# Products of constants around the norm sums of a two-block transformer kernel, in PSUM areas that nothing reads

## What is computed

```
def rms_norm(x, g):
    xf = x.astype(jnp.float32)
    y = xf * lax.rsqrt(jnp.mean(xf * xf, axis=-1, keepdims=True) + EPS)
    return y.astype(x.dtype) * g
...
    def pre(t, mm, i, gi):
        return rms_norm(t, g[gi]) * (1 + mm[:, :, i + 1]) + mm[:, :, i]

    def post(t, y, mm, i, gi, wres):
        return t + wres * mm[:, :, i + 2] * rms_norm(y, g[gi])
...
    for i in range(DEPTH):
        h = _rmsnorm(x, norm_g[i, 0])
        ...
        x = x + _rmsnorm(h, norm_g[i, 1])
        f = _conv_ffn(_rmsnorm(x, norm_g[i, 2]), ffn_w_up[i], ffn_conv_w[i], ffn_conv_b[i], ffn_w_down[i])
        x = x + _rmsnorm(f, norm_g[i, 3])
```

## Time and profile before

| | |
|---|---|
| median of three runs | 2756.01 us |
| profiled execution | 2758.69 us, its span 2756.9 us |
| TensorE matmul records | 2623.8 us busy, 95% of the span |
| VectorE (DVE), ScalarE (ACT) | 1558.1 us and 1185.0 us |
| mean granted TensorE clock | 0.977 of full speed |
| DMA | 375.51 MB, mean 136 GB/s |

### The profile page before, as it was taken

The page is one execution under the profiler, slowest core; times in us unless marked ns, Lnnn a source line. Parts: engine busy times, 40 slices in busy tenths (PEclk is TensorE's granted clock), DMA queues, the critical chain, the costliest instruction groups (busy, mean ns, idle before and its releaser), DMA issues. The chain is left out here.

```text
span 2756.9 us, 38954 instructions
## 1 busy us (share of the span) xinstructions
PE 2623.8 (95%) x16089; PEld 2250.3 (82%) x16089; DVE 1558.1 (57%) x2180; ACT 1185.0 (43%) x1636; POOL 112.5 (4%) x174
## 2 busy tenths in 40 slices
PE   6999999999999998999999989989988899898998
PEld 4777786876677786888886879989977899887998
DVE  5777536455777634322336574456566676565675
ACT  4222226454422224422326454444556565453663
POOL 1111300000111000000200000000000000000000
PEclk9999999999999999999999999999999999899999
DMA  8666532212566523223423234544421455331553
GB/s 304 230 225 227 137 107 62 62 62 84 172 216 212 194 92 97 71 93 112 123 77 92 62 115 159 179 157 144 166 80 55 134 182 180 137 127 62 172 172 114
DMA packets 248077, 375.51 MB, mean 136 GB/s; under 512 B 9820, under 2 KB 188568, under 8 KB 247936
## 3 DMA queue, kind: packets, MB, share of 16 engines
q1 hardware_dynamic: 228592, 300.56, 32.7%
q0 software_dynamic: 18768, 70.85, 7.9%
q10 hardware_dynamic: 576, 2.10, 0.2%
HBM read 372.34 MB, written 1.16 MB: 135 GB/s over the span
## 5 line engine op out<-in xcount | busy, mean ns | idle before, releaser
L499 PE MATMUL ps<-uh,wh 128*128 128x256 f32 (+1 forms) x4128 | 1382.8, 335 | 53.5 <-DVE ul L896 32.6
L500 PE MATMUL ps<-ul,wh 128*128 128x256 f32 (+1 forms) x4128 | 1366.2, 331 | 0.0
L501 PE MATMUL ps<-uh,wl 128*128 128x256 f32 (+1 forms) x4128 | 1365.9, 331 | 0.0
L499 PEld LDWEIGHTS ps<-uh,wh 128*128 128x128 f32 x4128 | 792.5, 192 | 169.0 <-issue 54.6
L501 PEld LDWEIGHTS ps<-uh,wl 128*128 128x128 f32 x4128 | 792.3, 192 | 71.3
L500 PEld LDWEIGHTS ps<-ul,wh 128*128 128x128 f32 x4128 | 793.0, 192 | 67.9 <-issue 0.7
L490 DVE TENSOR_TENSOR wl<-ring,wh 128x2048 fp32r<-128x2048 f32 (+1 forms) x209 | 475.1, 2274 | 479.8 <-ACT wh L485 376.1
L485 ACT ACTIVATE wh<-ring 128x2048 fp32r<-128x2048 f32 x155 | 296.7, 1915 | 712.5 <-PE ps L501 708.9
L1238 DVE TENSOR_TENSOR wl<-ring,wh 128x2048 fp32r<-128x2048 f32 x66 | 151.3, 2292 | 300.4 <-ACT uh L1256 281.7
L762 DVE SCALAR_TENSOR_TENSOR arena<-arena,act_c 128x384 f32<-128x384 f32 x420 | 228.5, 612 | 88.0 <-DMA arena<-in_w_ada_dram 87.7
L1235 ACT ACTIVATE wh<-ring 128x2048 fp32r<-128x2048 f32 x66 | 126.4, 1915 | 335.7 <-PE ps L501 335.7
(11 more groups left out here) (367 smaller groups left out, 2198.5 us busy)
## 6 DMA issues: line engine op xcount, KB each, us to landing
ring<-in_ffn_wi_dram SPq DMA_DIRECT2D x88, 1024.0 KB, 7.5
arena<-in_w_ada_dram POOLq DMA_DIRECT2D x84, 768.0 KB, 5.4
ring<-in_ffn_w_up_dram SPq DMA_DIRECT2D x44, 1024.0 KB, 7.0
ring<-in_ffn_wo_dram SPq DMA_DIRECT2D x20, 2048.0 KB, 8.0
ring<-in_ab_w_in_dram SPq DMA_DIRECT2D x13, 2048.0 KB, 7.6
ring<-in_ffn_w_down_dram SPq DMA_DIRECT2D x10, 2048.0 KB, 7.7
ring<-in_c_w_in_dram SPq DMA_DIRECT2D x6, 2048.0 KB, 8.0
ring<-in_w_in_dram SPq DMA_DIRECT2D x20, 512.0 KB, 6.5
```

What stands on the lines that cost most here:

```text
L499: pe.matmul(to, sh, mh, start=start and n == 0, stop=False)
L500: pe.matmul(to, sh, ml, start=False, stop=False)
L501: mm = pe.matmul(to, sl, mh, start=False, stop=stop and last)
```

## The change

A method `keep_busy` issues n products of the ones matrix with 256 columns of constants (the identity and the ones matrix). `Norm.tensor` calls it ahead of the sums unless the stage has begun with other products (the latent ones pass `begun=True`): six with 512 columns, into bank 2, four with 256 columns, into columns 256 to 511 of bank 7. With 512 columns it calls it again behind the sums, six into bank 0. Nothing reads the results. Since DVE still reads columns 0 to 255 of bank 7 with 256 columns, its multiply for k = 7 waits until the four are done. The method `done` counts the new semaphore on.

```diff
+        kept_busy = signal("products_between_done")
...
+            def keep_busy(self, pe, bank, n):
+
+                for _ in range(n):
+                    mm = pe.matmul(bank, ones, const[:, 0:S], start=True, stop=True)
+                return mm
+
-            def tensor(self, pe):
+            def tensor(self, pe, begun=False):
                 if self.post is None:
                     return
+                if not begun:
+                    if self.n_s == 2:
+                        self.keep_busy(pe, ps[:, 2, 0:S], 6)
+                    else:
+                        self.keep_busy(pe, ps[:, KD - 1, S:T2], 4).then_inc(kept_busy.sem, 1)
                 for k in range(KD):
                     pe.wait_ge(h_squared.sem, h_squared.at(k + 1))
                     last = pe.matmul(self.sum_bank(), ones, self.sq[:, k, :], start=(k == 0), stop=(k == KD - 1))
                 last.then_inc(sum_ready.sem, 1)
+                if self.n_s == 2:
+                    self.keep_busy(pe, ps[:, 0, 0:S], 6)
...
-                    self.post.vector(dve)
+                    self.post.vector(dve, (lambda: dve.wait_ge(kept_busy.sem, kept_busy.at(1))) if self.n_s == 1 else None)
...
-            def vector(self, dve):
+            def vector(self, dve, last_bank_free=None):
                 T = self.T
                 dve.wait_ge(y_rstd.sem, y_rstd.at(1))
                 for k in range(KD):
+                    if k == KD - 1 and last_bank_free is not None:
+                        last_bank_free()
...
-                    norm.tensor(pe)
+                    norm.tensor(pe, begun=True)
```

More of the change, by code:

```diff
@@ L928, in done @@
                 if self.post is not None:
+                    if self.n_s == 1:
+                        kept_busy.passed(1)
                     h_squared.passed(KD + 1)
```

## The result

| | before | after |
|---|---|---|
| median | 2756.35 us (8 runs, 2754.86 to 2761.11) | 2764.31 us (8 runs, 2757.56 to 2768.88) |
| ratio to before, 95% interval | | 1.0026 [1.0017, 1.0034] |
| profiled execution, span | 2758.69, 2756.9 us | 2765.02, 2763.2 us |
| mean granted clock | 0.977 | 0.984 |

The account below looks back on a forecast made before the run. The prediction took a stream of matmuls as the bound, with time lost where TensorE idles or runs at 1.2 GHz. Sums 3.0 plus wide first products 1.5 gave 4.5 us, hence 2751.5 us; 8-in-10 range 2746.5 to 2757.

Parts of the forecast that it names:

- Cost of the products: At the boundaries' gaps: 56 constant products, some 25 us of TensorE, fit into idle time; 0 on the path.
- DVE's wait: Ahead of DVE's eighth multiply (k = 7) at 256-column boundaries: the four products are done long before; cost 0.
- Sums: Sums at the nine boundaries: shorter idle ahead keeps the clock more often; gain 3.0 us, between 0 and 4.8.
- First products, wide: After the sums at 512-column boundaries: idle 4.68 becomes 2.0, three quarters of 2.1 us kept; gain 1.5, between -2.8 and 2.1.
- First products, narrow: After the sums at 256-column boundaries: 2.7 us idle stays, three of five lose the clock again; 0, between +4.1 and -2.8.
- rival C: 256-column boundaries: clock loss moves to the first products of all five, +2.8 us there; total about 2760 us; chance 0.10.
- C's other half: 256-column boundaries: the last sums still run at half speed, so the 3.0 us is not gained.
- Other clock losses: Dense work untouched by the change: clock losses can begin a little earlier or later; 0, plus or minus 1.5 us.
- the two places with narrow weight-bound products: 2398.60 to 2405.40 us, after products 32 columns wide with full TensorE records, and a like place near 1900.
- the three times shown: Run times of the kernel before, spread over only 2.5 us, taken to speak for a small part of chance.

## Why the prediction was wrong, point by point

**Cost of the products, DVE's wait: right.** 2.8 us for six, all in the gaps; the first product comes 4.64 us after the start of the Ln at boundary 2, as before, and the first sum 4.48 us after the end of the residual's sum, as before. No squares were late.

**Sums: the size nearly right, with two errors in it.** The term was 3.0. The Ln's wait fell by all of 5.0 us (15.3 to 10.3): the clock held under every sum, at the projections too, where I had given it three fifths. But at 6 and 8 the end of the sums is not what is late next. DVE at boundary 6, after:

```profile
1851.04 1.23 DVE L1770 TENSOR_TENSOR wl<-ring,wh 128x1024 fp32r<-128x1024 f32 x1
1852.17 2.29 DVE L491 TENSOR_TENSOR wl<-ring,wh 128x2048 fp32r<-128x2048 f32 x1
1854.37 1.28 DVE L903 SCALAR_TENSOR_TENSOR arena<-h,cols,rstd 128x256 f32<-128x256 f32 x3
```

Two pieces of weight splitting stand on DVE between the last update of `h` and the scaling, and end at 1854.4; 1/rms would have been there at 1853.4. Before, the slow sums hid them. Of 1.45 and 0.97 us gained, 0.96 went back at each; net 3.1. TensorE's idle stretch ahead of the first products grew by the same amount there, from 2.75 to 3.71 us. All 20 such places without products behind the sums lost their clock, ten with some 2.8 us of idle time and ten with 3.7.

**First products, wide: 1.5 forecast, 1.4 in the profile, at most 0.6 of it by the change.** Boundary 1 gave 0.8 and boundary 2 0.6. But at boundary 1 the 49th product starts 12.8 us after the first in the changed kernel, in the second profile of the unchanged program, and with nine products behind the sums at a clock of 1.00. So the 13.6 us of the profile on which the forecast rests were an unlucky case, and the change has no share in that gain. All that boundaries 1 and 2 gained, 0.8 and 0.6 in first products and 0.85 in sums, was given back at once: the stage between boundaries 2 and 3 took 375.3 us before and 377.5 after. TensorE's wait there for the modulation tiles that DVE folds, in the window 712:1086 of before and 709:1086 of after:

```profile
PE ps L778 <- DVE arena L762: 0.2, 1, 0.2
```

```profile
PE ps L779 <- DVE arena L763: 2.4, 4, 0.9
```

The seven profiles with products at the wide boundaries have 376.2 to 377.5 us in this stage, the six without them 374.9 to 375.7. That DVE and the loads of the modulation weights set a pace of their own there, for which an earlier TensorE waits, fits these numbers; no run tested it. The kernel with wide products alone made no difference in time (1.0005). And the products kept the clock less often than the three quarters I gave: in six profiles with six behind the sums, 16 of 24 wide boundaries still had low clock in their first products; with nine, none of four.

**First products, narrow: 0 forecast, +4.3 in the profile.** This step failed, and rival C named it, with a chance of 0.10 and 2.8 us. The forecast took which boundaries lose their clock to be drawn anew, three of five again. It is not drawn: in all five profiles without products at the narrow boundaries it is 5, 6 and 8 that lose, never 7 or 9. With four products ahead and none behind (five profiles), 5, 6 and 8 lost 14 of 15 times and 7 and 9 four of ten, 18 of 25 in all; the changed kernel's profile, with all five, is the worst of them (the others have three, three, three and four), and a loss there can cost more, 2.6 us at boundary 7. Four products behind removed most of it: 2 of 10 lost, both at projections, where 2.0 us of idle time were left (1.0 at the others), and 8.3 us in the median. C's other half, that the sums would stay slow, was wrong.

**Other clock losses: 0 plus or minus 1.5 forecast, +4.1 in the scans and +1.2 between 8 and 9.** This is the second step that failed, and the larger one. By the sizes in the profile, either loss alone leaves the median outside the range (2759.0 without this one, 2760.0 without the last); without both it would be 2754.7. I had seen that clock losses in dense work could start "a little earlier or later", and priced that by the two places with narrow weight-bound products; the scans I took as fixed. The three kernels that move nothing but the scans' start show the size: 0.9 us of added work made one 6.7 us slower and the other 4.3 us faster. The kernel before starts the scans at a cheap place, in two profiles 0.06 us apart. The three profiled kernels with the narrow sums sped up, nothing behind them and nothing else moved started at a dear one (129.3, 131.5 and 131.7 us); so did the one with wide products alone (132.8), in its longest execution. From the narrow spread of the three times shown I took chance to have a small part in it. That held for the kernel before only: the changed kernel's executions spread over 11 us. The measured +4.1 is one draw from that spread, and the forecast had no term for it.

What the Trainium skill says ("TensorE: Matmul & The Clock Gate", Part 1, What's actually happening), that the activity window runs free and doesn't start with the kernel, agrees with the profiles: at the start of the span the offset is 1.0, 1.0, 2.4 and 0.1 us in the four whose program is that of before up to the scans. The same section puts the penalty of the ramp at under 1% of a typical kernel's span and advises against fitting a model to a count of slow matmuls. The 6.7 us here are 0.2% of the span, so within that figure, but more than the whole gain that was forecast.

**How the kernel before comes to its place.** Nothing ties its start to the grid, and yet it reaches the scans at nearly the same offset. The profiles show that it is drawn there on the way. In those four the first product of boundary 1 has offsets of 1.4, 3.1, 2.7 and 2.1 us, that of boundary 3 0.2, 0.5, 0.1 and 0.3, that of boundary 6 3.3, 3.4, 3.3 and 3.3. The changed kernel is drawn less surely: in the three profiles of its program up to the scans (itself, with the scans moved, with varied values) boundary 6 has 2.8, 2.8 and 2.1. A low stretch ends on the grid and so may carry its place into what follows, which would explain it, but no run tested that.

**Left open.** The +1.2 us between 8 and 9 was not taken apart. How much of the 8.0 us in the medians belongs to the narrow first products and how much to the scans is known for the profiled execution alone.

## What to carry to other kernels

If a filler on TensorE is to pay, let it close every idle stretch up to the next real product: four products ahead of the narrow sums alone made this kernel slower (1.0017), four on each side faster (0.9983). Half a filler can move the low clock from work that waited anyway (sums behind DVE) to dense work behind it. Before crediting a gain at a boundary, find what is late next there and in the stage that follows (here DVE's weight splits and the modulation tiles). And where a later stage is sparse and clock-sensitive, a shift of under 1 us ahead of it can outweigh the edit; a control that adds only such a shift tells the two apart. Profile the unchanged program twice before you price what one profile lost: here 0.8 us of it was gone in the second.

## What the runs showed of the hardware that was not expected

- The same 858 matmuls took 124.6 to 132.8 us by the place in the clock's grid at which they began, with DVE and ACT unchanged.
- Products of ones and the identity went with a clock of 2.4 GHz through the sums of all nine boundaries of the changed kernel (the Ln waited 10.3 us in all, the full-clock value). Varied values did the same.
- An idle stretch of 2.1 to 2.2 us, between 2.75 us of products and the first real ones, still lost the clock in 16 of 24 cases; one of 2.0 in two of four; one of 1.0 or less in none of fifteen.
- Executions that began at different places of the grid, 0.1 to 2.4 us from its last point, reached boundary 6 within 0.1 us of the same place.
